# Rope ahead of the input tiles in the first chunk of a layer, its rows turned into a PSUM bank of their own

## What is computed

```python
mod = jax.nn.silu(c) @ w_ada + b_ada
shift, scale, gate = jnp.split(mod, 3, axis=-1)
h = rms_norm(x, g_pre) * (1.0 + scale[:, None, :]) + shift[:, None, :]
q_a, k_a, v_a, gate_a, q_i, k_i, w_i, q_b, k_b, v_b, gate_b = split_cols(h @ w_in)
...
q_i = rope(q_i.reshape(B, T, N_IDX, IDX_DIM), pos)
k_i = rope(k_i.reshape(B, T, 1, IDX_DIM), pos)[:, :, 0]
...
rel = jax.nn.relu(jnp.einsum('bqhd,bsd->bqhs', qi_b, ki))
score = jnp.einsum('bqhs,bqh->bqs', rel, wi_b) * IDX_SCALE     # then top-k keys, attention, retention
x = x + gate[:, None, :] * rms_norm(mixed @ w_out, g_post)
```

## Time and profile before

| | us |
|---|---|
| median of 3 runs (1498.38 to 1500.71) | 1499.03 |
| the profiled execution | 1496.76 |
| its span in the trace | 1495.0 |
| TensorE busy | 1399.0 (94%) |
| VectorE busy | 1047.0 (70%) |
| first `idx` chunk, first rope to the first `ret` rope | 52.27 to 137.13 |
| second `idx` chunk, likewise | 792.44 to 866.72 |

### The profile page before, as it was taken

One profiled execution on the slowest core, in us unless ns is written; L12 is line 12 of the kernel. 1 busy time (PEld: TensorE's weight loads), 2 busy tenths in 40 slices (PEclk: granted clock), 3 DMA queues, 4 the chain that ended last, 5 costly groups with the idle time before them and its releaser, 6 DMA issues.

```text
span 1495.0 us, 24410 instructions
## 1 busy us (share of the span) xinstructions
PE 1399.0 (94%) x7591; PEld 1064.4 (71%) x7591; DVE 1047.0 (70%) x3021; ACT 788.2 (53%) x1916; POOL 411.1 (27%) x360
## 2 busy tenths in 40 slices
PE   6779999999999999989996999999999999998996
PEld 2655777777877667658876577878888766765785
DVE  1697888999996556542397889999999655654224
ACT  2545666666316566564453566666622656565421
POOL 2541332433321011001287114444432101100100
PEclk9989999999999999999998999999999999999998
DMA  8412334332222112113252111111223211211324
GB/s 313 135 60 73 102 114 125 115 94 91 55 87 64 40 33 71 61 59 122 84 179 57 30 45 48 51 47 33 59 55 89 62 40 37 70 59 56 113 80 160
DMA packets 125191, 122.05 MB, mean 82 GB/s; under 512 B 33256, under 2 KB 94024, under 8 KB 125064
## 3 DMA queue, kind: packets, MB, share of 16 engines
q1 hardware_dynamic: 124608, 120.36, 26.1%
q10 hardware_dynamic: 456, 0.13, 0.0%
HBM read 93.55 MB, written 26.90 MB: 81 GB/s over the span
## 4 chain that ended last, share of the span: by engine, by line
PE 58%; DVE 27%; issue 5%; DMA 4%; ACT 4%; POOL 0%; DVEq 0%; ACTq 0%; SPq 0%
PE proj L937 11%; PE proj L938 11%; PE proj L940 10%; PE turn L916 8%; PE logit L964 6%; DVE U L1642 5%; PE out_bank L991 5%; DVE U L1832 2%; PE spare L964 2%; DMA U<-x_dram 1%; DVE probsT_more L1715 1%; DVE by_cos_sin L1580 1%; DVE by_cos_sin L1582 1%; DVE turned L1597 1%; DVE probsT_more L1717 1%
## 5 line engine op out<-in xcount | busy, mean ns | idle before, releaser
L937 PE MATMUL proj<-w_hi,h_hi 128*128 128x512 f32 (+2 forms) x1440 | 579.2, 402 | 3.6 <-POOL h_lo L1445 2.2
L938 PE MATMUL proj<-w_lo,h_hi 128*128 128x512 f32 (+2 forms) x1440 | 539.2, 375 | 0.0
L940 PE MATMUL proj<-w_hi,h_lo 128*128 128x512 f32 (+2 forms) x1280 | 481.2, 376 | 0.0
L1439 POOL TENSOR_TENSOR w_lo<-w_raw,w_hi 128x512 fp32r<-128x512 f32 (+2 forms) x160 | 207.5, 1297 | 791.7 <-ACT w_hi L1168 791.7
L937 PEld LDWEIGHTS proj<-w_hi,h_hi 128*128 128x128 f32 x1440 | 275.0, 191 | 63.2 <-issue 22.6
L938 PEld LDWEIGHTS proj<-w_lo,h_hi 128*128 128x128 f32 x1440 | 275.1, 191 | 31.2
L940 PEld LDWEIGHTS proj<-w_hi,h_lo 128*128 128x128 f32 x1280 | 243.3, 190 | 37.2
L1642 DVE TENSOR_SCALAR_CACHE_REDUCE U<-score,cand 128x384 bf16<-128x384 f32 x310 | 222.6, 752 | 2.2
L964 PE MATMUL logit<-keys,queries 64*128 64x512 f32 (+4 forms) x454 | 140.6, 556 | 13.3 <-ACT U L1299 10.0
L1279 ACT ACTIVATE probsT_more<-turn 128x512 f32<-128x512 f32 (+3 forms) x156 | 76.3, 492 | 122.3 <-PE turn L916 89.4
L916 PEld LDWEIGHTS turn<-ident,U 128*128 128x128 f32 x672 | 79.6, 143 | 66.0 <-issue 50.5
(11 more groups left out here) (184 smaller groups left out, 2129.2 us busy)
## 6 DMA issues: line engine op xcount, KB each, us to landing
w_raw<-in_w_in_dram SPq DMA_DIRECT2D x80, 256.0 KB, 3.2
probsT_more<-in_w_ada_dram SPq DMA_DIRECT2D x64, 256.0 KB, 3.8
score<-mixed_dram SPq DMA_DIRECT2D x36, 256.0 KB, 2.8
score<-in_w_ada_dram SPq DMA_DIRECT2D x32, 256.0 KB, 4.9
w_raw<-in_w_out_dram SPq DMA_DIRECT2D x32, 256.0 KB, 3.3
U<-in_x_prompt_dram SPq DMA_DIRECT2D x14, 512.0 KB, 4.1
mixed_dram<-U SPq DMA_DIRECT2D x24, 192.0 KB, 2.1
gates_dram<-U SPq DMA_DIRECT2D x18, 256.0 KB, 2.2
```

The source lines that it names most:

```text
L937: nc.tensor.matmul(out, h_hi[:, k, tile], hi, start=(k == 0), stop=False)
L938: ins = nc.tensor.matmul(out, h_hi[:, k, tile], lo, start=False, stop=(t == SAMPLE and k == KT - 1))
L940: ins = nc.tensor.matmul(out, h_lo[:, k, tile], hi, start=False, stop=(k == KT - 1))
L1439: nc.gpsimd.tensor_tensor(w_lo[:, s % WS, 0:w], w_raw[:, n % RAWS, 0:w], w_hi[:, s % WS, 0:w].bitcast(F32), ALU.subtract).then_inc(w_lo_re ...
```

## The change

In the steps of an `idx` chunk, and there only:

- VectorE ropes first and takes the hidden tile after it, one half in quarter 0 and one in quarter 1. In layer 0 the take moves from the end of step i-1 to after the rope of step i; in layer 1 from ahead of the rope of step i to behind it. `norm_input` moves from the end of a step to quarter 0 of the next, between the two halves. Ahead of the loop `norm_input(2)` moves behind `take_hidden(0, 1)`.
- The roped rows are turned into `out_bank` with two semaphores of its own instead of into the ring of `turn0` and `turn1`.
- ScalarE makes the high part of the hidden tile behind the quarters and ahead of `take_projection`, and the high part of the weights after quarter 1.
- GpSimd makes the low part of the weights ahead of that of the hidden tile in layer 0.

```diff
@@ weight slices, the rings
+def weight_slice_at(i):
+
+    return weight_slice(i + 1) if i + 1 < STEPS else None
...
-                if kind(i) in ("idx", "ret", "att"):
+                if kind(i) in ("ret", "att"):
                     turns.append(("q", i))
...
+IDX_TURN_AT = {("q", g): n for n, g in enumerate(k for k in range(STEPS) if kind(k) == "idx")}
...
         turns = Ring(turn_banks, TURN_AT, turn_full, turn_taken)
+        idx_turns = Ring([out_bank], IDX_TURN_AT, [idx_turned], [idx_turn_taken])
...
+        def turns_of(g):
+
+            return idx_turns if kind(g) == "idx" else turns
@@ ScalarE
             for i in range(-1, STEPS + 2):
-                for l, t in hidden_turns(i - 1):
-                    if l == 0:
-                        split_hidden(l, t)
-                if i + 1 < STEPS:
-                    if weight_slice(i + 1) is not None:
-                        split_weights(weight_slice(i + 1))
+                if i < 0:
+                    split_hidden(0, 1)
+                if weight_slice_at(i) is not None and kind(i) != "idx":
+                    split_weights(weight_slice_at(i))
                 for q in range(QUARTERS):
...
                     middle(i - 1, q)
+                    if q == 1 and weight_slice_at(i) is not None and kind(i) == "idx":
+                        split_weights(weight_slice_at(i))
...
+                for l, t in hidden_turns(i - 1):
+                    if i >= 0 and kind(i) == "idx":
+                        split_hidden(l, t)
                 if i + 1 < STEPS:
                     take_projection(i + 1)
                 for l, t in hidden_turns(i - 1):
-                    if l:
+                    if kind(i) == "out":
                         split_hidden(l, t)
@@ GpSimd
+                if weight_slice_at(i) is not None:
+                    lower_weights(weight_slice_at(i))
                 for l, t in hidden_turns(i - 1):
                     if l == 0:
                         lower_hidden(l, t)
-                if i + 1 < STEPS and weight_slice(i + 1) is not None:
-                    lower_weights(weight_slice(i + 1))
@@ VectorE
-            norm_input(2, mean_squares(2 + XLAG, 1, 2))
+            unit = mean_squares(2 + XLAG, 1, 2)
             take_hidden(0, 1)
+            norm_input(2, unit)
...
                 if roots_input(i) is not None:
-                    unit = mean_squares(roots_input(i) + XLAG, 1, 2)
+                    input_units[roots_input(i)] = mean_squares(roots_input(i) + XLAG, 1, 2)
                 for l, t in hidden_turns(i - 1):
-                    if l:
+                    if l and kind(i) != "idx":
                         take_hidden(l, t)
...
+                    if i >= 0 and kind(i) == "idx" and q < 2:
+                        for l, t in hidden_turns(i - 1):
+                            take_hidden(l, t, (q,))
+                    if q == 0 and roots_input(i - 1) is not None:
+                        norm_input(roots_input(i - 1), input_units[roots_input(i - 1)])
                     if kind(j) == "idx":
                         weigh_relus(j, q)
...
-                for l, t in hidden_turns(i):
-                    if l == 0:
-                        take_hidden(l, t)
-                if roots_input(i) is not None:
-                    norm_input(roots_input(i), unit)
```

23 lines of the change are left out of this document (13 added, 10 removed).

## The result

| | before | after |
|---|---|---|
| median (lowest to highest), us, 12 runs each | 1499.98 | 1504.09 (1502.55 to 1508.17) |
| ratio, 95% interval | | 1.0031 [1.0022, 1.0039] |
| span of the profiled execution | 1495.0 | 1503.6 |
| second mean to first `ret` rope, layer 0 | 43.19 to 137.13: 93.9 | 44.17 to 147.85: 103.7 |
| mean ahead of the first rope to first `ret` rope, layer 1 | 788.75 to 866.72: 78.0 | 799.87 to 876.00: 76.1 |

The change makes the kernel slower, by 4.1 us between the medians and by 0.31% [0.22, 0.39] in the ratio; 1495.8 was forecast, and the range ended at 1501.5. The stretch between them (651.6 and 652.0 us) and the one behind them, up to VectorE's last addition (624.2 and 623.6 us), are alike.

What follows compares the result with a forecast made beforehand. TensorE, busy 94% of the span, was taken as the bound, but a chain of handovers in the early `idx` steps. Layer 0 +1.3 and layer 1 -4.5 gave -3.2 us: 1499.03 to 1495.8 us, range 1491.0 to 1501.5.

Steps and rivals of the forecast that it cites:

- Part 1: Both layers: VectorE's waits on the turned tile go, 2.04 us in layer 0's steps 0 to 2, 8.11 in layer 1.
- Part 2: Layer 0, up to rope 4: the loop through the input load takes 8.53 us; rope 4 comes 1.0 us later.
- the right ring: Layer 0's loop of norm, input load, ScalarE's squares, mean, rope and half the modulation: 8.53 us a step.
- Part 3: Layer 0, rope 4 to rope 7: 31.1 + 3.3 - 3.0 = 31.4 us, making +1.3 us for layer 0.
- recovered contention: Layer 0, rope 4 to rope 7: 3.0 of 7 us lost to GpSimd come back, bounds none and 5.
- The upper bound: Layer 0 at +5 us: the load loop takes 9.2 us a step and no contention with GpSimd is recovered.
- Part 4: Layer 1: no loop through a load, 5.4 us a step plus GpSimd's hold-ups; -4.5 us, between -2.2 and -8.1.
- eight of twelve GpSimd instructions at 0.85: Layer 1, rope 90 to rope 94: eight of GpSimd's twelve instructions cost VectorE 0.85 us each, 6.8 us.
- the bound of -2.2: Layer 1: the smallest gain allowed, the rope's own lead alone, 2.2 us.
- Part 5: Both idx chunks: own bank and moved weight slices cost nothing; a late low part would cost TensorE 1.3 us once.
- The load ring and GpSimd dominate: Slower rival: load loop 9.2 us or more, nothing recovered, layer 0 +5, layer 1 -2.5; 1501.5 us, chance 0.20.
- signs of being wrong: Mean does not wait, early ropes over 9 us apart, or layer 1's first `ret` rope gains under 3 us on layer 0's.

Runs made afterwards that it cites:

- poolback: The changed kernel with GpSimd's low part of the weights behind that of the hidden tile again; 1501.65 us, 1.0006 of the kernel before.
- led0: The kernel before with the change in layer 0 alone, the bank of its own in both layers; 1506.87 us, 1.0060 of the kernel before.
- outbank: The kernel before with only the turned rows in a bank of their own, no instruction moved; 1499.74 us, 0.9990 of the kernel before.
- psrc_before: The kernel before with the two rope products of the idx chunks reading PSUM instead of ScalarE's SBUF copy; 1509.59 us, 1.0074 of the kernel before.
- nolock: The changed kernel with GpSimd's low parts written as zeros in idx steps, leaving out that computation; 1488.58 us, 0.9915 of the kernel before.
- pfull_all3: The changed kernel plus third input slot, mean behind rope and norm, low weights last, rope products and head weights read from PSUM; 1487.36 us, 0.9917 of before.
- led1_ring: The kernel before with the change and the bank of its own in layer 1 only; 1498.94 us, 0.9995 of the kernel before.

## The prediction against this

- **Part 1 held.** The waits on the turned tile went in both layers.
- **Part 2** drew the right ring. Ahead of the loop -0.8 was forecast, and the way from the second mean to rope 0 went from 9.08 to 8.24 us. The ring's size failed: 8.53 without the low weights on the rope (poolback: 8.7), 9.57 with them. From rope 0 to rope 3 that is 28.7 us against 23.0, +5.7 where 2.6 was forecast. The prediction named that very hold-up, with 9.2 us, and kept it for the rival.
- **Part 3** failed in its recovery. From rope 4 to rope 7 31.4 was forecast and 34.2 came. The 3.0 us of recovered contention did not come: if each VectorE instruction but the modulations is set against its shortest of that shape, 7.1 us were lost to hold-ups in this stretch before and 6.7 after. The upper bound, nothing recovered (34.4), is what the profile shows. VectorE idles only 0.3 us there, so TensorE's waits for the low parts do not set it. They come out behind rope 7, in a term that the sum had not: from rope 7 to rope 8 VectorE idles 4.5 us against 1.8 before, mostly for relus of a TensorE that is late and at a clock of 0.88, and the step is 2.8 us longer (1.3 in led0). Since the clock alone moves this place by 3 us, I take the size from medians: led0 is +6.9, where +1.3 was forecast for layer 0, and the changed kernel +4.1, where -3.2 was.
- **Part 4** was right in mechanism and wrong in size: 5.5 us a step without low parts, 7.3, 7.6 and 8.6 with them. The term "eight of twelve GpSimd instructions at 0.85" is the one that was too small: three ropes alone exceed 1.62 by 2.0, 2.3 and 3.4 us, and all hold-ups between ropes 90 and 94, counted as in part 3, are 9.5 us where 6.8 was put down (4.7 before). So rope 94 led by 0.3 us instead of 2.2, counted from the mean, and TensorE's further lead was worth 1.6 us up to the first `ret` rope instead of 2.3. -4.5 was forecast, -1.8 came, just outside the bound of -2.2.
- **Part 5 held**: the bank and the moved weight slices cost nothing that outbank or the traces show.
- **The rivals.** "The load ring and GpSimd dominate", given 0.20, is what happened, past its own number of 1501.5, since it still let layer 1 gain 2.5 and bounded layer 0 at +5. The sum erred where it took the middle of the contention in both layers and left the low weights off the rope in the ring; it did not use where GpSimd's low parts stood in the early steps, at 62.58 just as the rope ended. The steps that failed are therefore three terms: the ring's 8.53 us (9.57), the 3.0 us recovered (0.4) and the 6.8 us held up in layer 1 (9.5).
- **The signs.** The mean waits and a load is under way in that time, as forecast. Two of the three signs of being wrong came: early ropes over 9 us apart, and a first `ret` rope of layer 1 that gains 1.4 us on that of layer 0, where less than 3 was the sign. What the prediction calls steps 4 and 5 (85.6 to 97.0) is step 4 alone; nothing hangs on it.

## What to carry to other kernels

When a step that frees a buffer is moved behind another in a loop, close the ring on paper through the load and everything that stands ahead of the freeing step in the next turn, and open it (a slot more, or the consumer later) in the same change. Where VectorE and GpSimd meet, read who arrives first at present: a fast sequence may be fast because it holds the other engine back, and taking one operand out of it can cost more than it saves. Gains of that kind may only show together: here the new order, the open rings and the PSUM operand gave 0.8% (0.6% with the low weights first). The new order with only one of the other two gave at most 0.2%, and the old order with one of them nothing; the old order with both was not run.

## What the hardware showed unexpectedly

- A VectorE instruction of four columns with one operand in SBUF took 0.16 us alone, 1.16 to 1.22 us beside GpSimd's subtraction (psrc_before, after) and 0.59 us beside a GpSimd memset of 0.52 us (nolock). With its operand in PSUM it took 0.15 us beside the subtraction (pfull_all3).
- A tiny GpSimd power (128x1) took 0.55 us beside a rope whose products read PSUM (psrc_before). Beside the rope of two SBUF operands it took 0.73 or 1.14 us, in steps 0 and 1 of the kernel before, although it began 0.16 us behind the rope's start both times.
- The same 36 matmuls of one step took 6.50 us (before) or 9.52 us (led1_ring), at a granted clock of 1.00 and 0.71, each time behind a wait of TensorE of 2.10 us on ScalarE; in the second the clock stayed at 1.2 GHz for part of the step.
